# Samples' key scores on TensorE, the attention loop right behind the top-k, and the division of probabilities on ScalarE

## What is computed

```python
def select_keys(qi, wi, ki, qpos, topk):
    s = jnp.einsum('bqhd,bsd->bqhs', qi, ki) * IDX_DIM ** -0.5      # 8 index heads of 32
    score = jnp.einsum('bqhs,bqh->bqs', jax.nn.relu(s), wi * N_IDX_HEADS ** -0.5)
    score = jnp.where(kpos[None, None, :] <= qpos[None, :, None], score, -jnp.inf)
    _, idx = lax.top_k(score, topk)
    return idx, idx <= qpos[None, :, None]

def attend(q, kg, vg, valid):
    logits = jnp.einsum('bqhd,bqkhd->bqhk', q, kg) * HEAD_DIM ** -0.5
    logits = jnp.where(valid[:, :, None, :], logits, -jnp.inf)
    p = jax.nn.softmax(logits, axis=-1)
    return jnp.einsum('bqhk,bqkhd->bqhd', p, vg)

def layer(x, ...):
    u = rms_norm(x, g_pre_mix)
    q, k, v, qi, ki, wi, bx, gb, gc, glu, zg, xbc, dt = split(u @ w_in)
    y_a = sparse attention;  y_b = gb * dwconv3(gc * bx)
    y_c = silu(layer_norm(dwconv31(ga * sigmoid(gg))));  y_d = Mamba-2 scan of silu(dwconv4(xbc)), gated by silu(zg)
    x = x + rms_norm(concat[y_a, y_b, y_c, y_d] @ w_out, g_post_mix)
    ...   # feed-forward
```

## Time and profile before

| | |
|---|---|
| median of 3 runs | 1547.42 us (1546.89 to 1548.22) |
| profiled execution, its own time | 1550.66 us |
| its span in the profile | 1549.1 us |
| PE busy | 1424.0 us (92%) |
| DVE busy | 844.8 us (55%) |
| ACT busy | 537.3 us (35%) |
| POOL busy | 203.1 us (13%) |
| layer 1, features to the end of the loop | 103.6 to 276.5 us |
| layer 2, the same | 865.2 to 1037.7 us |

### The profile page before, as it was taken

The page is one execution under the profiler, slowest core; times in us unless marked ns, Lnnn a source line. Parts: engine busy times, 40 slices in busy tenths (PEclk is TensorE's granted clock), DMA queues, the critical chain, the costliest instruction groups (busy, mean ns, idle before and its releaser), DMA issues. The chain is left out here.

```text
span 1549.1 us, 28682 instructions
## 1 busy us (share of the span) xinstructions
PE 1424.0 (92%) x11510; PEld 1319.7 (85%) x11510; DVE 844.8 (55%) x1729; ACT 537.3 (35%) x879; POOL 203.1 (13%) x138
## 2 busy tenths in 40 slices
PE   4999878997999999999769998799989999999995
PEld 4889864897999999999657997558979999999994
DVE  5489998735444444222446898976264443442224
ACT  3443234444322222222344422445342232222222
POOL 1334312020000000000040442311200000000010
PEclk8999988999999999999879998999999999999997
DMA  6443231221333332233055333212313233323221
GB/s 222 133 133 96 80 85 44 97 86 44 94 94 95 88 88 83 76 93 93 9 201 146 104 87 88 81 40 87 96 55 95 84 92 95 92 64 94 84 73 55
DMA packets 222718, 141.20 MB, mean 91 GB/s; under 512 B 13514, under 2 KB 218674, under 8 KB 222102
## 3 DMA queue, kind: packets, MB, share of 16 engines
q1 hardware_dynamic: 220006, 132.57, 29.0%
q0 software_dynamic: 2624, 7.48, 1.3%
HBM read 124.66 MB, written 11.77 MB: 88 GB/s over the span
## 5 line engine op out<-in xcount | busy, mean ns | idle before, releaser
L1861 DVE TENSOR_TENSOR w_lo<-ring,w_hi 128x1024 fp32r<-128x1024 f32 (+2 forms) x164 | 179.3, 1093 | 399.2 <-ACT w_hi L1247 399.2
L623 PE MATMUL PS<-u_hi,w_hi 128*128 128x260 f32 x1600 | 325.5, 285 | 15.4 <-DVE u_lo L1982 11.7
L1247 ACT CAST w_hi<-ring 128x1024 fp32r<-128x1024 f32 (+2 forms) x168 | 158.9, 946 | 473.3 <-PE PS L623 473.3
L623 PE MATMUL PS<-u_hi,w_lo 128*128 128x260 f32 x1600 | 322.4, 283 | 0.0
L623 PE MATMUL PS<-u_lo,w_hi 128*128 128x260 f32 x1408 | 283.8, 283 | 0.0
L623 PEld LDWEIGHTS PS<-u_hi,w_hi 128*128 128x128 f32 x1600 | 246.8, 189 | 18.8 <-issue 13.0
L623 PEld LDWEIGHTS PS<-u_hi,w_lo 128*128 128x128 f32 x1600 | 247.4, 189 | 0.0
L623 PEld LDWEIGHTS PS<-u_lo,w_hi 128*128 128x128 f32 x1408 | 218.3, 189 | 0.0
L623 PE MATMUL PS<-hid_hi,w_hi 128*128 128x260 f32 x704 | 141.8, 283 | 3.6 <-ACTq L1404 3.6
L623 PE MATMUL PS<-hid_hi,w_lo 128*128 128x260 f32 x704 | 141.8, 283 | 0.0
L623 PE MATMUL PS<-hid_lo,w_hi 128*128 128x260 f32 x704 | 141.4, 282 | 0.0
(11 more groups left out here) (346 smaller groups left out, 2192.2 us busy)
## 6 DMA issues: line engine op xcount, KB each, us to landing
ring<-in_ffn_gate SPq DMA_DIRECT2D x44, 512.0 KB, 3.7
ring<-in_ffn_up SPq DMA_DIRECT2D x44, 512.0 KB, 3.7
ring<-in_w_in SPq DMA_DIRECT2D x36, 512.0 KB, 3.6
ring<-in_ffn_down SPq DMA_DIRECT2D x32, 384.0 KB, 3.4
ring<-in_ffn_down SPq DMA_DIRECT2D x32, 320.0 KB, 3.0
ring<-in_w_out SPq DMA_DIRECT2D x16, 512.0 KB, 4.1
x_store<-x SPq DMA_DIRECT2D x2, 2080.0 KB, 15.4
x<-x_store SPq DMA_DIRECT2D x2, 2080.0 KB, 7.8
```

Of the source, the lines that this page charges most:

```text
L623: ins = pe.matmul(to[:, h, :], w[:, k - base, :], a[k][:, h * HALF:(h + 1) * HALF], start=(begin and w is whi and a is a_hi), stop=(end an ...
L1247: act.copy(w_hi[part % 2][:, 0:n, :], raw[part % 4][:, 0:n, :]).then_inc(part_hi, 1)
L1861: dve.tensor_tensor(w_lo[part % 2][:, 0:n, :], raw[part % 4][:, 0:n, :], w_hi[part % 2][:, 0:n, :].bitcast(F32), ALU.subtract).then_inc(pa ...
```

## The change

Four things are changed together. (1) The scores of cached keys: PE turns each sample's keys (32 transposes, `keys_turn`) and index keys (4 transposes in `keys_prepare`, with 8 small ones and 4 small products for the queries and the index weights), ACT copies them into SBUF, and PE multiplies the queries with them (`index_logits`, `key_products`, `index_scores`); DVE only prepares masked query columns (`keys_prepared`, inside its top-k rounds) and copies the scores. `spread` and DVE's eight products go. The rows of the samples' logits now stand 32 partitions apart, on 128 partitions in two rows of 257, so mask, softmax and turns of the probabilities work on that shape. (2) The loop starts after 5 and a third tiles instead of 11, and each of its 16 steps holds two parts of 16 products. (3) ACT divides the probabilities with a scaled copy; DVE only takes the reciprocal. (4) The samples' steps, convolutions, states, tails and taps stand at other steps, and the slabs come in another order.

```diff
-        FEAT_SLABS = [5, 4, 3, 6, 7, 8, 2, 0, 1]
+        FEAT_SLABS = [4, 6, 7, 8, 3, 2, 0, 5, 1]
...
-        SPREAD_FROM = 7
         PER_TILE = 6 * KC
-        PER_SPREAD = PER_TILE // 2
+        PER_PART = PER_TILE // 3
         TAIL_TILES = 2
-        STEP_PRODUCTS = (14, 12, 13, 9, 13, 9, 13, 9, 13, 9, 9)
-        LOOP_TILES = SPREAD_FROM + NS * PER_SPREAD // PER_TILE
-        DENSE_STEPS = 11
+        LOOP_TILES = 5
+        LOOP_FIRST = LOOP_TILES * PER_TILE + PER_PART
...
-        STATES_FROM = 13
+        STATES_FROM = 11
...
-        TAP_SETS = {12: 2, 13: 3, 14: 3, 15: 3, 16: 3, 17: 2}
+        TAP_SETS = {15: 4, 16: 4, 17: 8}
...
+            return PER_PART if 0 <= j < len(STEPS) else 0
...
+                    def keys_prepare():
+                        pe.wait_ge(turned_ready, 7)
+                        pe.wait_ge(rope_done, 5)
+                        pe.wait_ge(ki_cache_in, 16 * 2 * NS)
+                        for t in range(NS // 2):
+                            last = pe.transpose(bank(4)[:, t * P:(t + 1) * P],
+                                                ki_cache[:, 4 * t:4 * t + 4, :].rearrange("p i c -> p (i c)"), ident)
+                        last.then_inc(key_pe, 1)
...
-                    def spread(b):
+                    def keys_turn(b):
+                        if b == 0:
+                            pe.wait_ge(k_cache_in, 16 * 2 * NS)
                         if b >= 2:
-                            pe.wait_ge(rows_used, b - 1)
-                        pick = ident_r[0:NS, b:b + 1].broadcast_to([NS, P])
-                        for part, lo, to in ((rows_hi[:, 0:W], rows_lo_q, bank(4 + 2 * (b % 2))[:, 0:W]),
-                                             (rows_hi[:, W:SPREAD_W], rows_lo_i, bank(5 + 2 * (b % 2))[:, 0:SPREAD_W - W])):
-                            pe.matmul(to, pick, part, start=True, stop=False)
-                            last = pe.matmul(to, pick, lo, start=False, stop=True)
-                        last.then_inc(rows_spread, 1)
+                            pe.wait_ge(keys_kept, b)
+                        for c in range(2):
+                            for pg in range(2):
+                                last = pe.transpose(bank(6 + b % 2)[:, c * W + pg * P:c * W + (pg + 1) * P],
+                                                    k_cache[:, 2 * b + pg, c * P:(c + 1) * P], ident)
+                        last.then_inc(key_pe, 1)
...
+                    def index_logits():
+                        pe.wait_ge(queries_kept, 1)
+                        pe.wait_ge(keys_kept, 1 + NS)
+                        for q in range(2):
+                            for pg in range(2):
+                                for g in range(4):
+                                    b = 4 * q + g
+                                    r = 32 * (b % 2 * 2 + pg)
+                                    last = pe.matmul(bank(5 + 2 * pg)[32 * g:32 * g + IH, q * P:(q + 1) * P],
+                                                     qi_cols[r:r + 32, :, b], ki_turned[r:r + 32, (b // 2) * P:(b // 2 + 1) * P],
+                                                     start=True, stop=True)
+                        last.then_inc(key_logits, 1)
+                    def key_products(q):
+                        pe.wait_ge(keys_kept, 1 + 4 * (q + 1))
+                        for c in range(2):
+                            for g in range(4):
+                                b = 4 * q + g
+                                last = pe.matmul(bank(4)[32 * g:32 * g + HEADS, q * W:(q + 1) * W], q_cols[:, c, b, :],
+                                                 k_turned_of[b][:, c * W:(c + 1) * W], start=(c == 0), stop=(c == 1))
+                        if q:
+                            last.then_inc(key_logits, 1)
+                    def index_scores():
+                        pe.wait_ge(logits_kept, 2)
+                        pe.wait_ge(keys_kept, 1 + NS)
+                        for q in range(2):
+                            last = pe.matmul(bank(6)[0:NS, 0:W], wi_cols[:, q, :], idx_part[:, q * W:(q + 1) * W],
+                                             start=(q == 0), stop=(q == 1))
+                        last.then_inc(dec_pe, 1)
...
-                    feature_products((SPREAD_FROM - 2) * PER_TILE)
-                    pe.wait_ge(turned_ready, 7)
-                    pe.wait_ge(rows_lo_ready, 2)
+                    feature_products(PER_PART)
+                    keys_prepare()
                     for b in range(NS):
-                        spread(b)
-                        feature_products(PER_SPREAD)
...
+                        if b in (0, 2, 4, 6):
+                            feature_products(PER_PART)
+                        keys_turn(b)
+                    index_queries()
+                    feature_products(PER_PART)
+                    index_logits()
+                    key_products(0)
+                    feature_products(PER_PART)
+                    key_products(1)
+                    feature_products(LOOP_FIRST - feat_i[0] - PER_PART)
+                    index_scores()
+                    feature_products(PER_PART)
...
+                        for b in range(NS):
+                            q, r = b // 4, 32 * (b % 4)
+                            last = pe.matmul(bank(2 + q)[r:r + 32, 0:261], ident[0:NS, b:b + 1].broadcast_to([NS, 32]),
+                                             m_row[0:NS, :], start=True, stop=True)
...
+                    pe.wait_ge(conv_c_done, 1)
                     cumulate(0)
...
+                    act.wait_ge(key_pe, 1)
+                    act.copy(ki_turned, bank(4)).then_inc(keys_kept, 1)
+                    for b in range(NS):
+                        act.wait_ge(key_pe, b + 2)
+                        act.copy(k_turned_of[b], bank(6 + b % 2)).then_inc(keys_kept, 1)
+                        if b == 3:
+                            feature_out(3)
                     feature_out(4)
...
+                    act.wait_ge(key_prep, 2)
+                    act.copy(qi_cols.rearrange("p h b -> p (h b)"), bank(5)[:, 64:128]).then_inc(queries_kept, 1)
+                    act.wait_ge(key_logits, 1)
+                    for pg in range(2):
+                        act.activation(idx_part.rearrange("p (q g k) -> p q g k", q=2, g=2)[:, :, pg],
+                                       bank(5 + 2 * pg)[:, 0:W].rearrange("p (q k) -> p q k", q=2), ACT.Relu).then_inc(logits_kept, 1)
+                    act.wait_ge(key_logits, 2)
+                    act.activation(l_row[:, :, 0:W], bank(4).rearrange("p (q k) -> p q k", q=2), ACT.Copy, scale=const("row_used"))\
+                       .then_inc(logits_kept, 1)
                     feature_out(LOOP_TILES)
...
+                        if 1 <= j <= len(STEPS):
+                            i = j - 1
+                            keys = (STEPS[i][0] + 1) * P
+                            act.wait_ge(denom_turned, i + 1)
+                            act.activation(rect[:, i % 2, 0:keys], rect[:, i % 2, 0:keys], ACT.Copy, scale=rden[:, i % 2:i % 2 + 1])\
+                               .then_inc(prob_ready, 1)
...
                             dve.wait_ge(exp_done, i + 1)
-                            step(dve.reciprocal(rden[:, b2], denom[:, b2]))
-                            settle()
-                            dve.tensor_scalar(rect[:, i % 2, 0:keys], rect[:, i % 2, 0:keys], rden[:, b2], None, ALU.mult)\
-                               .then_inc(prob_ready, 1)
+                            dve.reciprocal(rden[:, b2], denom[:, b2]).then_inc(denom_turned, 1)
...
                         if j == 0:
                             self_scores()
                         elif j == 1:
+                            dve.wait_ge(dec_dve, 1)
+                            decode_best(TOPK_SAMPLE // 16)
                         elif j == 2:
                             decode_best(TOPK_SAMPLE // 16)
                             decode_mask()
+                        elif j == 3:
+                            softplus()
                         elif j == 4:
+                            decode_logits()
                         elif j == 5:
+                            decode_probs()
                             conv_d_samples()
                         elif j == 6:
                             conv_d(0)
                         elif j == 7:
+                            decode_columns()
                             conv_d(1)
                         elif j == 8:
+                            gate_c()
+                        elif j == 9:
                             conv_d(2)
+                        elif j == 10:
+                            state_rows()
                             conv_d(3)
+                        if j == 15:
+                            conv_b(0)
+                        if STATES_FROM <= j < STATES_FROM + NS // 2:
+                            sample_states(j - STATES_FROM)
+                        if j == 11:
```

(13 more changed lines are left out.)

284 lines of the change are left out of this document (133 added, 151 removed).

## The result

The changed kernel takes 1554.4 us (median of 20, 1549.4 to 1559.1) against 1548.9 for the kernel before in the same rounds: ratio 1.0037, 95% interval 1.0028 to 1.0046. It is slower, by 5.4 us.

The account below looks back on a forecast made before the run. PE, busy for 92% of the span, was taken as the bound: its work, idle time and clock loss. A layer: 5.5 + 2.3 - 1.9 = +5.9, two layers +12, so 1547.42 + 12 = 1559 us; range 1532 to 1574.

Parts of the forecast that it names:

- +12: Whole program, two layers at +5.9 us each: slower, 1559 us; own range 1551 to 1567, chance 0.50.
- tile switches: In the loop, PE waits for ACT's tile copy: nine of 0.3 to 1.8 us, two hidden, one 2.6; 10.9 us.
- Idle time: PE's waits from the features to the loop's end: 19.5 us a layer after the change, against 17.2 before.
- the logits': Ahead of the loop, PE waits 1.9 us at the index logits for ACT's copy of the index queries.
- the long wait: At step 13 of the loop, PE waits 4.7 us for DVE, with low part 15 and tap weights back to back.
- DVE is never late: Rival: the 6.4 us of waits at steps 12 and 13 and 4 us of clock go; 1538 us, faster chance 0.30.
- PE's work: From the features to the loop's end: 9.3 us added, 2.1 for cuts, 5.9 removed; net 5.5 us a layer.
- 10 cuts, 2.1 us: Feature products on PE split into 42 pieces instead of 32, each cut costing about 0.2 us; bounds 0 and 4.
- The clock: PE's loss at a lower clock from the features to the loop's end: 6.0 us a layer instead of 7.9.
- it cancels: Rival: the terms cancel and nothing can be told, within 0.2%, 3 us; chance 0.08.
- The eight DVE products: DVE's products with cached keys beside a busy PE: worth nothing by themselves, but the loop may start earlier.
- The division: In the loop, moved to ACT: DVE loses 16 scalings, 7.2 us, and the 3.1 us of waits on L1813 go.

Follow-up runs that it names:

- e1: The changed kernel with the tap weights on POOL behind low part 13 in place of 15: 1550.1 us, ratio 1.0012 to the kernel before.
- e11: The changed kernel, unaltered, profiled a second time: 1552.6 us, one execution.
- e2: The changed kernel with the index logits one piece later, behind the first half of the key products: 1550.9 us, ratio 1.0015 to the kernel before.
- e7: The changed kernel with ACT copying a finished feature tile ahead of the cast of the next weights: 1542.8 us, ratio 0.9962 to the kernel before.
- e9: The changed kernel with tap weights behind low part 13, index logits one piece later and ACT's tile copy ahead of its cast: 1540.1 us, ratio 0.9947.
- e12: The kernel before, unaltered, profiled a second time: 1549.7 us, one execution.
- e6: The changed kernel with nine and a third tiles ahead of the loop, 10 products a part, POOL's other work shifted to fit: 1577.7 us, ratio 1.0191.
- e3: The changed kernel with the division of the probabilities back on DVE: 1553.3 us, ratio 1.0037 to the kernel before.
- e4: The kernel before with only the division moved, DVE taking the reciprocal and ACT making the scaled copy: 1551.2 us, ratio 1.0023.
- e10: The changed kernel with tap weights behind low part 13, index logits one piece later, copy ahead of cast, and division on DVE: 1537.6 us, ratio 0.9920.

## Why the prediction was right, and where its sizes were off

It said slower, 1559 us with 1532 to 1574 as the range, from +12; measured is +5.4. The sign and the waits were right, two sizes of the sum were not. In its count of tile switches nine, two and one make twelve, where eleven tiles end in the loop.

- **Idle time** was forecast 19.5 us a layer and is 17.7, with each of its items within 1.1 us of its forecast. The cause of the long one is shown by layer 2 of e1 and by e11, that of the logits' by e2, that of the switches by e7. The forecast took the long wait as certain; it is there in three layers of four, and where it is not, idle time is 15.4 us. The rival "DVE is never late" is out.
- **PE's work** was forecast to grow by 5.5 us a layer and grew by 2.6 to 3.0 (table). The rows of the new key path:

```profile
130.36 1.03 PE L762 MATMUL PS<-cst,side 128*128 128x128 f32 x8
131.32 0.32 PE L750 MATMUL PS<-arena,cst 128*32 128x64 f32 x8
...
135.55 0.66 PE L775 MATMUL PS<-side 32*8 32x128 f32 x32 [1.79 <-ACT side L1270]
136.14 0.44 PE L786 MATMUL PS<-side 128*4 128x256 f32 x4
...
140.78 1.05 PE L786 MATMUL PS<-side 128*4 128x256 f32 x16
141.76 0.51 PE L722 MATMUL PS<-u_hi,w_lo 128*128 128x260 f32 x2
...
145.79 1.03 PE L796 MATMUL PS<-arena,side 128*8 128x256 f32 x4
146.75 0.39 PE L722 MATMUL PS<-u_hi,w_hi 128*128 128x260 f32 x1
```

Eight turns take 0.96 us up to the index queries (130.36 to 131.32), eight key products 0.98 (140.78 to 141.76; each is two instructions here). The index logits take 0.59 instead of 1.2 (135.55 to 136.14), the index scores 0.96 instead of 0.3 (145.79 to 146.75); all added operations together 9.1 us at full clock, for 9.3, and all that went 5.8, for 5.9. The term that was mis-sized is "10 cuts, 2.1 us". By the trace of layer 1 the products of features stand in 25 unbroken pieces before and 30 after, not in 32 and 42: where nothing stands between two parts, they are one piece. So there are five cuts more, not ten. At full clock, from each product's start to the next instruction's, they take 97.1 us before and 96.7 after. A piece between two spreads cost 0.17 to 0.20 us over 0.121 a product, as priced, but the four new pieces ahead of two samples' turns each cost 0.06 to 0.09. So a cut does cost something; wrong were their number and the price of the new ones, and the term as a whole was nothing instead of 2.1 us a layer.
- **The clock** was forecast to lose 6.0 us in a stretch instead of 7.9, and lost 6.4 and 6.6 (5.0 and 6.4 in e11): right within its variation. What no step had is the fall behind the loop: in the 9 profiles of the changed kernel and its variants with five tiles ahead, 11 of 18 layers have one of 1.5 to 1.7 us where the output projection begins; in the 4 profiles of the kernel before and its variants, none of 8. In the profiled run it cost 1.5 + 1.6 us. What in the changed order brings it about is open: PE's instructions from the loop's end to there are the same in kind, PE's wait there is as long before (1.82 us) as after (1.84), and e9, with the same order behind the loop, has it in one layer only.
- **The sum**, for both layers: 5.4 (first profiles) to 6.0 us (e11 against e12) of work in the stretches, idle time there between +1.5 and -0.4, the clock there -3 to -5, and the clock behind them +3: about 5 us, and 5.4 measured. Over the whole program, with the clock in windows of 4 us, the first profiles differ by +4.8 of work, -1.6 of idle time and +4.1 of the clock's loss, together 7.3 us of span, the second by +4.7, -0.9 and -0.8, together 3.0. What repeats is PE's work. The rival "it cancels" was nearer than I thought (0.37% with a bound of 0.2%).
- **Costs at nothing.** The eight DVE products were worth nothing by themselves, as said; but I didn't price the early start that their removal allows. By e6 it is worth 23 us, in a kernel that has the key path and this order of steps. What the change paid for it is 5.4 to 6.0 us of PE's work and the waits.
- **The division** was said to win the 3.1 us of waits on L1813. It wins nothing (e3) or loses 3 us (e4): in e4 the waits for the probabilities went from 3.1 us in three places to 3.8 in five when the scaling moved to the engine that makes the exponential.

## What to carry to other kernels

A reordering that frees an engine pays only where what it frees is the late one at the next meeting: the same exchange of two ACT operations was worth 11.6 us in the changed kernel and nothing in the kernel before. When a change brings more hand-overs, look first at the order of operations in a hand-over (who waits for which of them), and at what GpSimd does back to back beside VectorE. A wait that rests on half a microsecond between two engines' starts can be there in one layer and not in the next, so look at both, and at the unaltered kernel twice, before you credit an edit. And a change that comes out slower may be a few small repairs away from the better structure: e10, with the three and the division back on DVE, is 16.8 us below the changed kernel and 11.8 below the one before (ratio 0.9920 on its own chip).

## What the runs showed of the hardware

- fp32 products with few output rows, written to four different groups of 32 partitions, take 0.12 us each with 256 columns (L786, eight in 0.98); two that share their output rows take 0.48 each (L796). No run changes the output rows alone.
- The granted clock of one program falls at different places from execution to execution: the changed kernel lost 37.7 us of the whole span in one profile and 33.8 in the next (windows of 4 us), with the same work at full clock (1395.2 and 1394.8). Removing idle time didn't remove these losses: with 15.7 us less idle time over the whole program than the changed kernel, e9 lost 37.4 us to the clock.
- GpSimd's hold on VectorE adds up over operations back to back, if the first starts early enough: three convolution steps of 2.32 us took 7.64 with two that started 0.49 us behind them, 4.32 with two that started 0.93 behind (e7, layer 1) or with one 0.51 behind (e1, layer 2), and 2.32 with two that started 2.04 behind (e11, layer 2). GpSimd is held in turn: the tap weights took 4.13 us in the first case and 3.70 in the last.
- A fall of the clock can shorten idle time by moving one engine's start past another's: 15.4 us in layer 2 of e11, with a fall to 0.57 at 991 to 995, where the other layers of the changed kernel have 17.7.
